# Both attentions take the second token tile's units first and the first token tile's units last

## The chip, the core and the metric

The kernel runs on one core of a Trainium2 chip. The metric is the device time of one execution, in microseconds (us). TensorE (PE) multiplies matrices, VectorE (DVE) does elementwise work and reductions, ScalarE (ACT) does activations and copies out of PSUM, and SyncE (SP) issues the loads of weights. Every engine takes its instructions in program order and waits on semaphores for the others.

## The reference, cut to what matters

Two blocks of a transformer run one after the other on 256 tokens of width 1024. The first block has a mixer of two attentions (a forgetting attention with 8 heads, "fox", and a sparse attention with the branches "cmp", "slc" and "win" over 2 groups of 4 heads) and a feed-forward layer that retrieves experts. The second block has a banded attention with 16 heads and sinks, and a gated delta rule. Both attentions work on blocks of 128 queries and are causal:

```python
def block(i):                       # i = 0, 1: 128 queries each
    q0 = i * Q_BLOCK
    logits = einsum(q[q0:q0+128], k) * scale + (c_t - c_s)   # fox
    p = softmax(where(k_pos <= q_pos, logits, NEG_INF))
    return einsum(p, v)
out = lax.map(block, jnp.arange(S_ // Q_BLOCK))

# second block: keys within 128 positions, 16 meta tokens, and a sink logit
p = softmax(concat([s_band - slope * dist, s_meta - slope * dist, sink]))
o = p_band @ v_band + p_meta @ v_meta
```

No block of queries depends on another, so their order is free.

## The kernel before

The 256 tokens are two tiles of 128 (`NT` is 2). A unit of `attention_stage` is one token tile, one kind and one group of heads: for each tile two fox units (four heads each), one cmp unit (eight heads, 15 keys), and slc, win, slc, win (four heads each). That makes 14 units, numbered u = 0 to 13. The first tile can see only 128 keys, the second tile 256. So a fox, slc or win unit of the first tile has 128x512 scores, called a **short unit** here, and one of the second tile 128x1024, a **long unit**. A cmp unit has 128x120 in either tile.

Each engine runs a hand-written pipeline over the units.

- PE, at index u: the scores of unit u+2 (L734 and L739 for fox, L746 for slc and win, L728 for cmp); the merge tile u (L232 with the weights' high part, 16 matmuls, and L236 with the low part, 8), which is a piece of another projection with a weight tile of its own; the values of unit u-1 (L778; fox and win units only, a win unit's for all three branches); and the turning (transpose) of unit u (L763, L758 for cmp).
- DVE: peaks(u) is the masked copy out of PSUM (L835, for cmp L831 before it), the maximum (L839) and its negative (L845); scale(u-1) is a reciprocal and products (L859, L865, L873); then the low part of a weight tile (L192, in `make_low`).
- ACT: four exponentials of unit u (L895), the high part of that weight tile (L180, in `make_high`), the copy of the merge tile out of PSUM (L314), the copy of the values (L917, `store`), and the copy of the turned unit u-1 (L907, L904 for cmp).

The waits that matter are these. The exponentials wait for peaks(u). `make_high` comes behind them on ACT, and it also waits until PE has used the high part of merge tile u-1, because the high and low parts have two buffers each. `make_low` waits for `make_high`, and peaks(u+1) comes behind `make_low` on DVE. So one step of the pipeline is a loop from DVE to ACT and back to DVE, and PE joins it by the use of the merge tile.

The stage ends when the last values are stored. Then all engines pass to `merge_stage` (L976, L989), which needs the output of all units.

`sink_attention_stage` has 16 units, one per token tile and pair of heads, with 144 keys in the first tile and 272 in the second. Its pipeline is the same in kind: scores L1627, half of a gate tile L275, values L1652, turning L1639; peaks L1680 to L1693 and scale L1699 to L1704; exponentials L1721 and L1724, copies L1732 and L1735, store L1605, and the gates' opening L1610. A weight tile's halves are made in every second unit. It shares its program block with `out_rows` (L3095), so engines go on without a barrier.

Of the kernel before, what the change touches and what calls it, by code (L numbers as in the profile page):

```python
# [20 lines left out]
NT = S // P  # L21
# [20 lines left out]
AH = 16  # L42
# [636 lines left out]
def attention_stage(k):  # L679
# [8 lines left out]
    ahead = [k.tiles["merge_rest"] + i for i in range(AHEAD, rest)] + list(early(k, "branch"))  # L688
    fill = ps[:, 7, 0:S]
    units = []  # L690
    for tt in range(NT):
        units += [(tt, "fox", 0), (tt, "fox", 1), (tt, "cmp", 0)]
        units += [(tt, b, g) for g in range(2) for b in ("slc", "win")]
    n_exp = [0]
# [880 lines left out]
def sink_attention_stage(k):  # L1575
# [10 lines left out]
    high, low = k.pair(L)  # L1586
    fill = ps[:, 7, 0:L]
    value_bank = lambda u: 6
    units = [(tt, a) for tt in range(NT) for a in range(AH // 2)]
    keys = lambda tt: META + (tt + 1) * P  # L1590
    soft, pt = k.soft2, k.pt2
    st = k.small[:, 0:24].rearrange("p (s a h) -> p s a h", s=2, a=6)
# [289 lines left out]
def second_block(k, stop):  # L1882
# [21 lines left out]
    with k.joined():  # L1904
        last_values = sink_attention_stage(k)
        k.split_early.add(k.tiles["attn_out"])
        opened, stored = k.signals["gate_opened"], k.signals["att_stored"]
        out_rows(k, "attn_out",
                 [(k.hm, 0, META, 0)] + [(k.h[:, tt, :], 2 + 2 * tt, P, META + tt * P) for tt in range(NT)],
                 k.y2, k.tiles["dn_in"] + RING, k.T2[:, 10:18, :], lambda q: opened.at(q + 1), following="dn_in",  # L1910
                 scale=[None] + [k.norms[:, 24 + 3 + tt:24 + 4 + tt] for tt in range(NT)],
                 gate_on=lambda q: stored.at(8 + 2 * q + 2), rest_by_scalar=last_values)
# [1037 lines left out]
def first_block(k, stop):  # L2950
# [29 lines left out]
    end_early(k, "merge_rest")  # L2980
    if stop <= 3: return
    attention_stage(k)
    end_early(k, "branch")
    if stop <= 4: return
# [242 lines left out]
```

## Time and profile before

| what | value |
|---|---|
| time, median of 3 runs (lowest, highest) | 1673.17 us (1672.14, 1673.53) |
| the profiled execution's own time | 1672.73 us |
| span in the profile | 1671.0 us |
| mean granted TensorE clock | 0.991 |
| PE busy | 1609.6 us (96%) |
| DVE busy | 1169.1 us (70%) |
| ACT busy | 906.4 us (54%) |
| first attention, from the first scores to the last store | 114.7 to 205.5 us |
| second attention, from the first scores to the last store | 1175.4 to 1241.7 us |

The profile is one execution. Its times count from the first instruction, and 1.7 us of the execution lie outside the span. A granted clock of 1.00 is TensorE's full 2.4 GHz, 0.50 is its lower level of 1.2 GHz.

### The profile page before, as it was taken

The numbers are of one execution on the slowest core, as the hardware profiler recorded it, in microseconds if no ns is written. First come the engines' busy times: TensorE is split into PE (matmuls) and PEld (weight loads), VectorE is DVE, ScalarE is ACT, GpSimd is POOL, SyncE is SP. The second block draws the span as 40 slices with busy tenths as digits, with TensorE's granted clock in tenths as the row PEclk, the third lists the DMA queues.
The fourth block names the chain that finished last, engine by engine and source line by source line (L and its number), as shares of the span: only waits on it lengthen the run. The fifth ranks groups of instructions, "written<-read, shape, count | busy, mean of one in ns | idle before, by whom it ended". The sixth has DMA issues, their size and how long they took to land. (4 is left out here: it accounts for less than half of the span.)

```text
span 1671.0 us, 33887 instructions
## 1 busy us (share of the span) xinstructions
PE 1609.6 (96%) x12980; PEld 1437.5 (86%) x12980; DVE 1169.1 (70%) x2011; ACT 906.4 (54%) x1621; POOL 74.1 (4%) x41
## 2 busy tenths in 40 slices
PE   7989899999999999999999999999999999999998
PEld 6888788999999999998888888887667889888877
DVE  5656666688988999986666666655765757756565
ACT  4336654455555776666656666653564655334543
POOL 0000000200000000000000000000001333200000
PEclk9979999999999999999999999999999999999999
DMA  6532254455555444446666666642222444310004
GB/s 216 186 114 89 79 174 151 156 186 164 182 183 164 139 129 138 135 133 201 192 197 189 193 195 190 195 141 86 76 69 84 150 150 155 104 38 3 3 31 147
DMA packets 63222, 230.02 MB, mean 138 GB/s; under 512 B 7024, under 2 KB 7280, under 8 KB 63104
## 3 DMA queue, kind: packets, MB, share of 16 engines
q1 hardware_dynamic: 63104, 228.37, 43.7%
q8 instruction: 83, 1.36, 0.3%
q14 instruction: 35, 0.29, 0.1%
HBM read 227.30 MB, written 1.05 MB: 137 GB/s over the span
## 5 line engine op out<-in xcount | busy, mean ns | idle before, releaser
L1097 DVE TENSOR_TENSOR tile_low<-weights,tile_high 128x1024 fp32r<-128x1024 f32 x252 | 307.9, 1222 | 141.4 <-ACT tile_high L1087 141.3
L1087 ACT ACTIVATE tile_high<-weights 128x1024 fp32r<-128x1024 f32 x252 | 268.1, 1064 | 134.0 <-issue 134.0
L180 ACT ACTIVATE tile_high<-weights 128x1024 fp32r<-128x1024 f32 x169 | 178.4, 1057 | 231.3 <-issue 56.6
L192 DVE TENSOR_TENSOR tile_low<-weights,tile_high 128x1024 fp32r<-128x1024 f32 x146 | 179.7, 1233 | 140.7 <-ACT tile_high L180 128.6
L1169 PE MATMUL banks<-parts,tile_high 128*128 128x256 f32 x2048 | 272.0, 286 | 0.9 <-ACT tile_high L1087 0.6
L1169 PEld LDWEIGHTS banks<-parts,tile_high 128*128 128x128 f32 x2048 | 255.5, 193 | 1.7 <-issue 1.7
L1489 PE MATMUL banks<-tile_high,parts 128*128 128x512 f32 x1024 | 253.0, 389 | 0.9 <-ACT parts L1447 0.9
L1489 PEld LDWEIGHTS banks<-tile_high,parts 128*128 128x128 f32 x1024 | 192.2, 188 | 40.9 <-issue 1.1
L232 PE MATMUL banks<-parts,tile_high 128*128 128x272 f32 (+1 forms) x1216 | 169.8, 293 | 4.4 <-PEq L2909 3.4
L232 PEld LDWEIGHTS banks<-parts,tile_high 128*128 128x128 f32 x1216 | 158.4, 192 | 14.1 <-issue 10.8
L1174 PE MATMUL banks<-parts,tile_low 128*128 128x256 f32 x1024 | 144.3, 284 | 4.1 <-DVE tile_low L1097 4.0
L1489 PE MATMUL banks<-tile_low,parts 128*128 128x512 f32 x512 | 136.8, 389 | 0.0
L1174 PEld LDWEIGHTS banks<-parts,tile_low 128*128 128x128 f32 x1024 | 132.0, 192 | 5.3 <-DVE tile_low L1097 5.3
L1489 PEld LDWEIGHTS banks<-tile_low,parts 128*128 128x128 f32 x512 | 96.1, 188 | 19.9
L1223 ACT ACTIVATE big<-banks 128x256 f32 (+1 forms) x71 | 47.1, 664 | 104.4 <-PE banks L1174 104.4
L236 PE MATMUL banks<-parts,tile_low 128*128 128x272 f32 (+1 forms) x608 | 87.9, 287 | 1.6 <-DVE tile_low L192 1.6
L1447 ACT ACTIVATE parts<-big 128x256 fp32r (+1 forms) x128 | 88.1, 689 | 0.0
L1239 ACT ACTIVATE rows<-rows,kept 128x128 f32<-128x128 f32 x256 | 80.1, 390 | 8.7 <-DVE rows L1343 8.7
L1508 DVE TENSOR_TENSOR parts<-big,parts 128x256 fp32r<-128x256 f32 x128 | 82.4, 644 | 1.8 <-ACT parts L1447 1.8
L236 PEld LDWEIGHTS banks<-parts,tile_low 128*128 128x128 f32 x608 | 80.4, 189 | 1.8 <-DVE tile_low L192 1.8
L1343 DVE TENSOR_TENSOR rows<-const,kept 128x1024 f32<-128x1024 f32 x64 | 76.9, 1218 | 0.0
L3095 PE MATMUL banks<-tile_high,parts 128*128 128x512 f32 (+1 forms) x288 | 71.3, 392 | 1.9 <-ACT parts L3027 1.9
(401 smaller groups left out, 2182.4 us busy)
## 6 DMA issues: line engine op xcount, KB each, us to landing
weights<-in_peer_u SPq DMA_DIRECT2D x128, 512.0 KB, 3.5
weights<-in_peer_v SPq DMA_DIRECT2D x128, 512.0 KB, 3.5
weights<-in_dn_in SPq DMA_DIRECT2D x49, 512.0 KB, 3.5
weights<-in_in_t SPq DMA_DIRECT2D x19, 512.0 KB, 3.5
weights<-in_attn_t SPq DMA_DIRECT2D x19, 512.0 KB, 3.5
weights<-in_in_m SPq DMA_DIRECT2D x16, 512.0 KB, 3.6
weights<-in_wq SPq DMA_DIRECT2D x16, 512.0 KB, 3.5
weights<-in_dn_out SPq DMA_DIRECT2D x16, 512.0 KB, 3.5
```

The costliest lines, as they stand in the source:

```text
L180: k.nc.scalar.activation(k.high[:, m % 2, :], k.ring.view(n), ACT.Copy).then_inc(*k.high_made.up())
L192: unit.tensor_tensor(k.low[:, m % 2, :], k.ring.view(n), k.high[:, m % 2, :].bitcast(F32), ALU.subtract).then_inc(*k.low_made[engine].up())
L232: ins = nc.tensor.matmul(out, high[:, c, :], rhs(c)[part], start=part + c == 0, stop=False)
L236: ins = nc.tensor.matmul(out, low[:, c, :], rhs(c)[0], start=False, stop=c == chunks - 1)
L1087: k.nc.scalar.activation(k.high[:, (s + j) % 2, :], k.ring.buf[:, j % RING, :], ACT.Copy).then_inc(k.high_made.sem, 1)
L1097: k.nc.vector.tensor_tensor(k.low[:, (s + j) % 2, :], k.ring.buf[:, j % RING, :], k.high[:, (s + j) % 2, :].bitcast(F32), ALU.subtract).th ...
L1169: ins = nc.tensor.matmul(ps[:, bank, 0:S], high[:, c, :], x[:, c, :], start=part + c == 0, stop=False)
L1174: ins = nc.tensor.matmul(ps[:, bank, 0:S], low[:, c, :], k.pair(S)[0][:, c, :], start=False, stop=c == KC - 1)
L1239: nc.scalar.activation(hot, hot, ACT.Copy, scale=k.chosenT[:, 2, Q * g + q:Q * g + q + 1]).then_inc(*scaled.up())
L1447: nc.scalar.activation(stage[:, j % STAGES, :], c_of(i, j), ACT.Copy).then_inc(staged.sem, 1)
L1489: ins = nc.tensor.matmul(ps[:, 4 + 2 * tt + half, :], c[:, j % STAGES, tt * P:tt * P + P], v[:, half, :], start=head and j + part == 0, st ...
L1508: nc.vector.tensor_tensor(stage_low[:, j % STAGES, :], c_of(i, j), stage[:, j % STAGES, :].bitcast(F32), ALU.subtract).then_inc(staged_low ...
```

## The change

In both stages the list of units is built with the token tiles in reverse. Everything else is unchanged: the same instructions with the same shapes, the same merge and gate tiles at the same index u, the same buffers and waits.

```diff
@@ attention_stage
-    for tt in range(NT):
+    for tt in reversed(range(NT)):
         units += [(tt, "fox", 0), (tt, "fox", 1), (tt, "cmp", 0)]
         units += [(tt, b, g) for g in range(2) for b in ("slc", "win")]
@@ sink_attention_stage
-    units = [(tt, a) for tt in range(NT) for a in range(AH // 2)]
+    units = [(tt, a) for tt in reversed(range(NT)) for a in range(AH // 2)]
```

PE at the start of the first attention, before. L734 and L739 are the scores of the two fox units, L728 those of the cmp unit, L232 and L236 merge tile 0, L763 the turning of unit 0.

```order
72 L734 MATMUL banks<-big 128x128 x4
73 L739 MATMUL banks<-big,const 128x128 x4
74 L734 MATMUL banks<-big 128x128 x4
75 L739 MATMUL banks<-big,const 128x128 x4
76 L728 MATMUL banks<-big 128x15 x8
77 L232 MATMUL banks<-parts,tile_high 128x256 x16
78 L236 MATMUL banks<-parts,tile_low 128x256 x8
79 L763 MATMUL banks<-const,big 128x128 x4
```

And after:

```order
72 L734 MATMUL banks<-big 128x256 x4
73 L739 MATMUL banks<-big,const 128x256 x4
74 L734 MATMUL banks<-big 128x256 x4
75 L739 MATMUL banks<-big,const 128x256 x4
76 L728 MATMUL banks<-big 128x15 x8
77 L232 MATMUL banks<-parts,tile_high 128x256 x16
78 L236 MATMUL banks<-parts,tile_low 128x256 x8
79 L763 MATMUL banks<-const,big 128x128 x8
```

The rows keep their places; the four groups of scores ahead of the first merge tile are now 256 keys wide, and the turning has eight matmuls for four.

PE in the middle of that stage, before. The merge tiles here are 5, 6 and 7; L778 x12 are the values of a win unit of the first tile, and the scores are those of the second tile's fox units and, last, of its cmp unit.

```order
100 L232 MATMUL banks<-parts,tile_high 128x256 x16
102 L778 MATMUL banks<-big 64x128 x12
103 L763 MATMUL banks<-const,big 128x128 x4
104 L734 MATMUL banks<-big 128x256 x4
106 L232 MATMUL banks<-parts,tile_high 128x256 x16
108 L763 MATMUL banks<-const,big 128x128 x4
109 L728 MATMUL banks<-big 128x15 x8
110 L232 MATMUL banks<-parts,tile_high 128x256 x16
112 L778 MATMUL banks<-big 64x128 x12
```

And after:

```order
100 L232 MATMUL banks<-parts,tile_high 128x256 x16
102 L778 MATMUL banks<-big 64x128 x20
103 L763 MATMUL banks<-const,big 128x128 x8
104 L734 MATMUL banks<-big 128x128 x4
106 L232 MATMUL banks<-parts,tile_high 128x256 x16
108 L763 MATMUL banks<-const,big 128x128 x8
109 L728 MATMUL banks<-big 128x15 x8
110 L232 MATMUL banks<-parts,tile_high 128x256 x16
112 L778 MATMUL banks<-big 64x128 x20
```

Here the wide values and turnings of the second tile now stand behind merge tiles 5 to 7, where those of the first tile stood, while the fox scores ahead of merge tile 6 are the narrow ones.

PE at the end of that stage, before: the last two merge tiles, the turning of units 12 and 13 (L763) and the values of the last two win units (L778).

```order
132 L232 MATMUL banks<-parts,tile_high 128x256 x16
133 L236 MATMUL banks<-parts,tile_low 128x256 x8
134 L778 MATMUL banks<-big 64x128 x20
135 L763 MATMUL banks<-const,big 128x128 x8
136 L232 MATMUL banks<-parts,tile_high 128x256 x16
137 L236 MATMUL banks<-parts,tile_low 128x256 x8
138 L763 MATMUL banks<-const,big 128x128 x8
139 L778 MATMUL banks<-big 64x128 x20
```

And after:

```order
132 L232 MATMUL banks<-parts,tile_high 128x256 x16
133 L236 MATMUL banks<-parts,tile_low 128x256 x8
134 L778 MATMUL banks<-big 64x128 x12
135 L763 MATMUL banks<-const,big 128x128 x4
136 L232 MATMUL banks<-parts,tile_high 128x256 x16
137 L236 MATMUL banks<-parts,tile_low 128x256 x8
138 L763 MATMUL banks<-const,big 128x128 x4
139 L778 MATMUL banks<-big 64x128 x12
```

The last turning and the last values have half and three fifths of their matmuls.

## Rows read from the trace of the kernel before

**Rows 1.** Busy time by stretch: us, then PE, PEld, DVE, ACT, POOL, PEclk, DMA.
```profile
152.89:191.34 38.45, 35.84 (x315) 30.86 (x316) 28.52 (x45) 24.80 (x63) 0.00 (x0) 1.00 0.27 83
```

**Rows 2.** Timeline, the steps: start, duration, engine, line, operation.
```profile
131.23 0.68 DVE L835 SCALAR_TENSOR_TENSOR big<-banks,big 128x512 f32<-128x512 f32 x1
136.65 0.68 DVE L835 SCALAR_TENSOR_TENSOR big<-banks,big 128x512 f32<-128x512 f32 x1
...
152.89 1.22 DVE L835 SCALAR_TENSOR_TENSOR big<-banks,big 128x1024 f32<-128x1024 f32 x1
...
159.81 1.22 DVE L835 SCALAR_TENSOR_TENSOR big<-banks,big 128x1024 f32<-128x1024 f32 x1
...
166.72 0.21 DVE L831 SCALAR_TENSOR_TENSOR big<-banks,big 128x60 f32<-128x60 f32 x1
...
170.60 1.22 DVE L835 SCALAR_TENSOR_TENSOR big<-banks,big 128x1024 f32<-128x1024 f32 x1
```

**Rows 3.** Timeline, the first attention's head and two later score groups.
```profile
119.45 0.69 DVE L835 SCALAR_TENSOR_TENSOR big<-banks,big 128x512 f32<-128x512 f32 x1 [0.69 <-PE banks L739]
...
121.16 3.62 PE L232 MATMUL banks<-parts,tile_high 128*128 128x256 f32 x16
...
126.09 0.72 PE L746 MATMUL banks<-big 64*128 64x128 f32 x8
...
127.09 0.21 DVE L831 SCALAR_TENSOR_TENSOR big<-banks,big 128x60 f32<-128x60 f32 x1
...
171.22 1.13 PE L746 MATMUL banks<-big 64*128 64x256 f32 x8
```

**Rows 4.** Busy time by stretch, around the fall and the rise of the clock.
```profile
110.00:112.00 2.00, 1.62 (x11) 1.30 (x10) 1.97 (x3) 0.75 (x3) 0.00 (x0) 0.69 0.78 258
...
122.00:124.00 2.00, 2.00 (x11) 2.00 (x11) 0.00 (x0) 0.76 (x4) 0.00 (x0) 0.50 0.00 0
124.00:126.00 2.00, 2.00 (x17) 1.93 (x16) 0.05 (x1) 1.14 (x2) 0.00 (x0) 0.89 0.00 0
```

**Rows 5.** Timeline, PE's pieces of a unit at full clock, one ACT row.
```profile
130.39 0.66 PE L763 MATMUL banks<-const,big 128*128 128x128 f32 x4
...
158.34 1.07 PE L728 MATMUL banks<-big 64*128 64x15 f32 x16
...
168.37 1.06 ACT L180 ACTIVATE tile_high<-weights 128x1024 fp32r<-128x1024 f32 x1 [0.21 <-PE banks L232]
...
170.20 1.09 PE L763 MATMUL banks<-const,big 128*128 128x128 f32 x8
...
190.48 2.18 PE L232 MATMUL banks<-parts,tile_high 128*128 128x256 f32 x16 [0.69 <-ACT big L314]
...
193.55 2.55 PE L778 MATMUL banks<-big 15*64 15x128 f32 x40
```

**Rows 6.** Timeline, the end of the first attention and the short counterparts.
```profile
126.20 0.60 ACT L907 ACTIVATE big<-banks 128x512 f32<-128x512 f32 x1
...
162.41 1.68 PE L778 MATMUL banks<-big 15*64 15x128 f32 x24
...
191.34 1.22 DVE L835 SCALAR_TENSOR_TENSOR big<-banks,big 128x1024 f32<-128x1024 f32 x1
...
201.44 1.02 ACT L907 ACTIVATE big<-banks 128x1024 f32<-128x1024 f32 x1 [0.46 <-PE banks L763]
...
205.12 0.39 ACT L917 ACTIVATE big<-banks 128x256 f32<-128x256 f32 x1 [2.65 <-PE banks L778]
```

**Rows 7.** Timeline, short and long copy and values of the second attention.
```profile
1195.24 0.38 ACT L1735 ACTIVATE big<-banks 128x256 f32<-128x256 f32 x1
...
1196.87 0.81 PE L1652 MATMUL banks<-big 16*64 16x128 f32 x8
...
1236.40 0.60 ACT L1735 ACTIVATE big<-banks 128x512 f32<-128x512 f32 x1
...
1240.35 1.02 PE L1652 MATMUL banks<-big 16*64 16x128 f32 x12 [1.17 <-ACT big L1735]
```

## The prediction

> **What bounds the kernel now.** I read the page first: TensorE is busy 96% of the span, but the change touches only the two attentions, 91 us and 66 us of it, so what counts is what ends last inside them. The view of busy time by stretch shows for the long units of the first attention 35.84 us of PE and 28.52 us of DVE in 38.45 us [rows 1]. Neither is idle for long and neither is full. Then I read the timeline of DVE for the distance between the starts of the masked copies, since each of them opens a step. A short step is 5.42 us (131.23 to 136.65), a long step 6.92 us (152.89 to 159.81), a cmp step 4.14 us in the first tile (127.09 to 131.23) and 3.88 us in the second (166.72 to 170.60) [rows 2, 3]. These equal lengths are the loop from DVE to ACT and back: masked copy, maximum, negative, four exponentials, high part, low part. So this loop is the bound in nearly all steps. PE runs beside it with little room. At the second tile's cmp unit ACT's high part waits 0.21 us for the merge tile's matmuls [rows 5], so there PE is already the later of the two.
>
> **The steps between head and tail.** The loop of unit u has only unit u's own copy, maximum and exponentials in it; scale(u-1) runs on DVE while ACT does exponentials. So a step costs by its own unit wherever it stands, and reversing the tiles permutes the sum. What doesn't permute are the ends: which unit stands where the clock is low, which one is last, and where PE's load collects.
>
> **The head of the first attention.** TensorE's granted clock is 0.50 from about 110.8 us to 124.4 us: the stretch 110 to 112 has a mean of 0.69, 122 to 124 has 0.50, 124 to 126 has 0.89 [rows 4]. The four fox score groups of units 0 and 1 fall into it. The trace has no 256-key group at half clock. At full clock a group with 128 keys takes 0.72 us and one with 256 keys 1.13 us, both rows of L746 [rows 3]; the extra 0.41 us is columns alone. At worst it doubles to 0.82 us, at best it stays 0.41 us, so the four cost between 1.6 and 3.3 us. I take 3.3, since the clock row says half speed. The start of peaks(1) then moves from 119.45 to 122.8. It is followed by a full long step, so peaks(2) starts at 122.8 + 6.9 = 129.7. Before, that was 127.09 [rows 3], because ACT's high part waited for the slow merge tile 0 (3.62 us, from 121.16), and a short step would have ended at 124.9. The wait that was there before swallows a part of the change. The head costs +2.6 us. PE's own path, 3.3 us later than before but with its last part at full clock, arrives at about the same time.
>
> **The middle.** From 129.7: the long cmp unit 3.88, four long steps 27.7, the two short fox steps 10.8, then peaks of the first tile's cmp unit at 172.1. By the loop alone peaks(10) would start 4.14 later, at 176.3. But here PE's load collects. Merge tile 12 started 0.86 us ahead of peaks(13), with no scores left ahead of it (190.48 against 191.34 [rows 5, 6]). In the new order merge tile 6 stands in the same place behind long units, with two narrow fox score groups ahead of it (1.4 us), and peaks(7) is at 161.3; so it starts at about 161.8. Up to merge tile 8 PE has two merge tiles of 3.07 us (190.48 to 193.55), the cmp scores 1.07, the last long win unit's values 2.55, one long turning 1.09, one short one 0.66, and a narrow score group 0.72 [rows 3, 5]. That is 12.2 us, about 12.0 as the pieces overlap by a few hundredths each. Merge tile 8 starts at 173.8 and its high part is used at 176.0. ACT's high part can only then begin, and from there to the next masked copy it is 2.23 us (168.37 to 170.60 [rows 2, 5]), which makes 178.2. So the first tile's cmp step is 1.9 us late: PE ends last there. After it the short steps need of PE 3.07 + 0.72 + 0.66 and half of 1.68 us of values (a win unit is every second one), 5.3 us against a loop of 5.42, so PE doesn't bound them. Three more short steps bring peaks(13) to 194.5, where it was 191.34 [rows 6]: +3.1 us.
>
> **The tail of the first attention.** Before, from peaks(13) to the end of the last store there are 191.34 to 205.51, 14.2 us [rows 6]. In it unit 13's pieces are in series. They become short: copy, maximum and exponentials -1.50 (6.92 less 5.42), turning -0.43 (1.09 to 0.66), ACT's copy -0.42 (1.02 to 0.60), values -0.87 (2.55 to 1.68) [rows 5, 6]. The sum is -3.2 us. The last merge tile, the same as before, remains in it. So the stage gives +3.1 - 3.2 = -0.1 us.
>
> **The second attention.** It has eight short and eight long units too, and its steps permute in the same way. The tail is what changes: the last copy 0.60 to 0.38 us, and the last values 1.02 to 0.81 us; out_rows stands behind these on PE, and PE waited 1.17 us for just this copy [rows 7]. That is -0.4 us. The head has only two score pairs of extra columns at low clock and DVE is then the longer one; I put it at 0, with half a microsecond either way.
>
> **Everything else** keeps its instructions and waits. SP's loads are released by the use of the same weight tiles at the same index, and move with them by a few microseconds at most.
>
> **The sum.** -0.1 - 0.4 = -0.5 us against the profiled execution's 1672.73 us gives 1672.2 us. That execution is 0.4 us under the median of the runs, 1673.17, and inside their spread. About 0.2% (3.3 us) is what a measurement of this kernel can tell from no change, so this forecast is no change.
>
> **The low clock, by work or by time.** The rows show the half clock lasting through four score groups, the cmp scores and most of merge tile 0, and ending at 124.4 [rows 3, 4]. If it ended after an amount of work, the new head would carry 3.3 us more of half-clock work, merge tile 0 would be used at about 128.1, and the head would be 0.6 us later than summed: 1672.8 us. The Trainium skill, in "TensorE: Matmul & The Clock Gate", section "Part 1: The HAM clock gate (the "warmup" mystery)", says that the slow phase is an amount of time and not a number of matmuls, and that it differs from run to run by where the hardware's free-running window stands. By that rule the end stays at 124.4 and the sum stays at 1672.2. No row here separates the two.
>
> **Rivals.**
>
> *A new thin stretch lets the clock fall ahead of the merge stage (slower).* The place is 195 to 206 us. PE has fewer turnings and values there in the new order, then waits for the last copy, the last store and the stage's end. If the clock falls as it did at 110.8, the merge stage starts at half clock for the same 13.6 us. The same shape, L232 x16, took 3.62 us there against 2.18 us at full clock [rows 3, 5], so 40% of 13.6 us is lost: +5.4 us, 1677.6 us. It decides from the point where the granted clock between 205 and 220 is below 1. For it: the clock did fall once in this part of the program. Against it: the old tail has the same waits, longer ones, and the short units fill PE more densely than the long ones did there.
>
> *PE catches up early (faster).* If PE isn't late at the cmp unit (-1.9), and the wide scores cost only their full-clock columns (1.6 in place of 3.3, -1.7), the tail's gain comes through: 1672.2 - 3.6 = 1668.6 us. For it: cmp waited only 0.2 us for PE before. Against it: the wide values and turnings all lie ahead of it now, and the half clock is in the rows.
>
> *PE stays late through the short half.* If the short steps take 5.9 us in place of 5.42, since scores, turning and values in PE's row wait for one another, the five of them behind the first tile's fox units cost +2.4: 1674.6 us. For it: that much PE work in a step leaves nearly no room. Against it: the steps in the trace of before are 5.42 to the hundredth in the short half, right behind the low clock, where PE was just as late.
>
> **How the numbers follow.** Forecast 0.70, PE late through the short half 0.12, PE early 0.10, clock falls 0.08. The range takes in the head's two bounds, the late PE and most of the early one: 1669.0 to 1675.6 us. Faster by over 0.2% 0.12, within 0.2% 0.78, slower 0.10: the rivals at 1668.6 and 1677.6 and a little more on each side.
>
> **What would show it.** The masked copies on DVE start near 122.8 (unit 1), 129.7 (unit 2), 161.3 (unit 7), 172.1 (unit 9), 178.2 (unit 10) and 194.5 (unit 13). The cmp step of the first tile is near 6 us and ACT's high part in it waits for L232. The last store ends near 205.4, and 11 us behind the last masked copy. The last values of the second attention start near 1239.9 where they started at 1240.35 [rows 7]. The forecast is wrong if the stage ends more than 2 us off, or if the granted clock falls where it was 1.00.

## The result and the profile after

The changed kernel took 1678.62 us (median of 8 runs, 1677.52 to 1680.13) against 1672.66 us before (8 runs beside them, 1670.90 to 1675.50). The ratio is 1.0029 with a 95% interval of 1.0017 to 1.0040: slower by 0.29%, where I had forecast no change at 1672.2 us and a range up to 1675.6 us. The profiled execution took 1677.52 us with a span of 1675.8 us, 4.8 us over the span before. Its mean granted clock is 0.986 (0.991 before).

Four differences make up the 4.8 us. From its first score matmul to its last store the first attention takes 93.6 us in place of 90.8: +2.8. From that store to the first L3095 it is 28.4 us in place of 26.4: +1.9. Between the end of L1489 and the first L1627 it is +1.4, and ahead of the first attention -1.4. The second attention adds nothing in this pair. Ahead of the first attention the two kernels are the same, so the -1.4 is a difference between two executions. The +1.4 is a stretch at low clock, which shows in the view of busy time by stretch, first of before and then of after:

```profile
1116.00:1118.00 2.00, 2.00 (x18) 2.00 (x17) 0.47 (x2) 0.47 (x1) 0.00 (x0) 1.00 0.00 0
```
```profile
1116.00:1118.00 2.00, 2.00 (x12) 2.00 (x10) 1.09 (x3) 1.15 (x3) 0.00 (x0) 0.50 0.63 244
```

The clock is 0.50 there from 1115.5 to 1119.0 us in the changed kernel.

The timeline of DVE in the changed kernel shows the masked copies that open the steps (they answer to [rows 2, 3, 6]); columns are start, duration, engine, line, operation.

```profile
117.42 1.23 DVE L835 SCALAR_TENSOR_TENSOR big<-banks,big 128x1024 f32<-128x1024 f32 x1 [4.45 <-PE banks L739]
121.44 1.23 DVE L835 SCALAR_TENSOR_TENSOR big<-banks,big 128x1024 f32<-128x1024 f32 x1 [1.33 <-PE banks L739]
129.88 0.21 DVE L831 SCALAR_TENSOR_TENSOR big<-banks,big 128x60 f32<-128x60 f32 x1
135.29 1.22 DVE L835 SCALAR_TENSOR_TENSOR big<-banks,big 128x1024 f32<-128x1024 f32 x1
...
162.93 0.68 DVE L835 SCALAR_TENSOR_TENSOR big<-banks,big 128x512 f32<-128x512 f32 x1
...
173.76 0.21 DVE L831 SCALAR_TENSOR_TENSOR big<-banks,big 128x60 f32<-128x60 f32 x1
...
179.75 0.68 DVE L835 SCALAR_TENSOR_TENSOR big<-banks,big 128x512 f32<-128x512 f32 x1
...
196.00 0.68 DVE L835 SCALAR_TENSOR_TENSOR big<-banks,big 128x512 f32<-128x512 f32 x1
```

Counted from the stage's first matmul (113.29; 114.7 before), unit 2 opens at 16.6 us in place of 12.4. Its step, the long tile's cmp, takes 5.41 us (129.88 to 135.29) where it was 3.88. The first tile's cmp step takes 5.99 us (173.76 to 179.75), where it was 4.14. The last step opens at 82.7 us in place of 76.6, and the tail is 10.9 us in place of 14.2.

PE, ACT and DVE in the head of the changed kernel, from the timeline:

```profile
113.29 2.08 PE L734 MATMUL banks<-big 64*128 64x256 f32 x8 [0.94 <-PEq L2909]
...
121.32 1.89 PE L728 MATMUL banks<-big 64*128 64x15 f32 x16
...
123.14 3.78 PE L232 MATMUL banks<-parts,tile_high 128*128 128x256 f32 x16
...
126.72 1.91 PE L236 MATMUL banks<-parts,tile_low 128*128 128x256 f32 x8
...
127.01 1.06 ACT L180 ACTIVATE tile_high<-weights 128x1024 fp32r<-128x1024 f32 x1 [0.77 <-issue]
...
128.73 1.23 DVE L192 TENSOR_TENSOR tile_low<-weights,tile_high 128x1024 fp32r<-128x1024 f32 x1 [3.27 <-PE banks L236]
...
133.05 1.06 ACT L180 ACTIVATE tile_high<-weights 128x1024 fp32r<-128x1024 f32 x1 [1.73 <-PE banks L232]
```

A wide score group takes 2.08 us at half clock. Merge tile 0 runs at half clock to its end, 128.63. ACT's high part starts only 0.09 us behind the end of its high part (126.92), with ACT idle for 0.77 us before it. DVE is idle for 3.27 us ahead of its low part. For most of that it waits for ACT's high part, done at 128.07; the last 0.6 us are the wait for merge tile 0's low part (L236). In the next step ACT waits 1.73 us for merge tile 1: PE is the late one there.

Busy time by stretch in the changed kernel, around the clock's rise and around the stage's end (columns as in [rows 1, 4]):

```profile
127.00:128.00 1.00, 1.00 (x7) 1.00 (x6) 0.00 (x0) 0.99 (x1) 0.00 (x0) 0.50 0.00 0
128.00:129.00 1.00, 1.00 (x6) 1.00 (x6) 0.27 (x1) 0.40 (x2) 0.00 (x0) 0.50 0.00 0
129.00:130.00 1.00, 1.00 (x9) 0.83 (x9) 1.00 (x2) 0.22 (x2) 0.00 (x0) 0.95 0.00 0
...
206.00:207.00 1.00, 0.50 (x10) 0.26 (x6) 0.00 (x0) 0.39 (x1) 0.00 (x0) 1.00 0.00 0
207.00:208.00 1.00, 0.00 (x0) 0.00 (x0) 0.00 (x0) 0.78 (x1) 0.00 (x0) 0.80 0.00 0
208.00:209.00 1.00, 0.58 (x3) 0.62 (x4) 0.70 (x1) 1.00 (x2) 0.00 (x0) 0.50 0.77 102
...
213.00:214.00 1.00, 1.00 (x6) 1.00 (x6) 0.00 (x0) 0.66 (x1) 0.00 (x0) 0.50 0.00 0
214.00:215.00 1.00, 1.00 (x9) 1.00 (x8) 0.67 (x1) 0.00 (x0) 0.00 (x0) 0.79 0.00 0
```

The clock rises at 129.1 us, 15.8 us into the stage (9.7 before), and it falls again at 207.6 and stays at 0.50 until 214.4, where it had been 1.00 before. The merge stage's first matmuls run in it, as the timeline of PE shows; the end of the tail stands above them:

```profile
204.82 1.68 PE L778 MATMUL banks<-big 15*64 15x128 f32 x24 [0.69 <-ACT big L907]
208.41 4.10 PE L976 MATMUL banks<-parts,tile_high 128*128 128x256 f32 x16 [1.92 <-ACT parts L989]
212.31 1.91 PE L982 MATMUL banks<-parts,tile_low 128*128 128x256 f32 x8
```

Sixteen L976 take 4.10 us here and 2.08 us two tiles later (217.07). The last values wait 0.69 us for ACT's last copy (1.11 us before) and are short, as forecast.

The second attention's values in the view of one line, before and after (count, shortest, median and longest in ns, first and last start). The first L1627 starts at 1175.5 before and 1180.2 after, so the last of these comes 65.6 us into the stage in both.

```profile
L1652 PE MATMUL banks<-big x160: 268/273/324, 1182.8 to 1241.1; 128*64 128x128 f32 x96, 16*64 16x128 f32 x64
```
```profile
L1652 PE MATMUL banks<-big x160: 268/273/324, 1189.7 to 1245.8; 128*64 128x128 f32 x96, 16*64 16x128 f32 x64
```

### The profile page after: what moved, and what is told of

It is laid out like the page before. It is cut to its first block and busy times, and to the rows that moved or that the text cites. A ratio compares the mean times of both kernels' runs of the same rounds, so it can differ in the third digit from the quotient of the medians.

```text
span 1675.8 us, 33887 instructions
## 1 busy us (share of the span) xinstructions
PE 1614.9 (96%) x12980; PEld 1441.6 (86%) x12980; DVE 1169.5 (70%) x2011; ACT 907.0 (54%) x1621; POOL 74.1 (4%) x41
## 5 line engine op out<-in xcount | busy, mean ns | idle before, releaser
L1489 PE MATMUL banks<-tile_high,parts 128*128 128x512 f32 x1024 | 253.0, 389 | 0.9 <-ACT parts L1447 0.9
L1489 PEld LDWEIGHTS banks<-tile_high,parts 128*128 128x128 f32 x1024 | 192.2, 188 | 40.8 <-issue 1.1
L232 PE MATMUL banks<-parts,tile_high 128*128 128x272 f32 (+1 forms) x1216 | 170.0, 293 | 4.8 <-PEq L2909 3.4
L232 PEld LDWEIGHTS banks<-parts,tile_high 128*128 128x128 f32 x1216 | 158.4, 192 | 14.0 <-issue 10.4
L1489 PE MATMUL banks<-tile_low,parts 128*128 128x512 f32 x512 | 136.8, 389 | 0.0
L1489 PEld LDWEIGHTS banks<-tile_low,parts 128*128 128x128 f32 x512 | 96.1, 188 | 19.9
L236 PE MATMUL banks<-parts,tile_low 128*128 128x272 f32 (+1 forms) x608 | 89.4, 290 | 1.6 <-DVE tile_low L192 1.6
L236 PEld LDWEIGHTS banks<-parts,tile_low 128*128 128x128 f32 x608 | 81.9, 192 | 1.8 <-DVE tile_low L192 1.8
L3095 PE MATMUL banks<-tile_high,parts 128*128 128x512 f32 (+1 forms) x288 | 71.3, 392 | 1.9 <-ACT parts L3027 1.9
```

The costliest lines, as they stand in the source:

```text
L232: ins = nc.tensor.matmul(out, high[:, c, :], rhs(c)[part], start=part + c == 0, stop=False)
L236: ins = nc.tensor.matmul(out, low[:, c, :], rhs(c)[0], start=False, stop=c == chunks - 1)
L1489: ins = nc.tensor.matmul(ps[:, 4 + 2 * tt + half, :], c[:, j % STAGES, tt * P:tt * P + P], v[:, half, :], start=head and j + part == 0, st ...
L3095: ins = nc.tensor.matmul(ps[0:rows, bank + half, :], xs[:, place(q), c0:c0 + rows][:, c, :], w[:, c, :], start=q + part + c == 0, stop=q = ...
```

## The experiments

All ratios are to the kernel before, timed in turn on the same chip. Executions of one and the same kernel spread over 2 to 11 us here (the kernel before over 5 to 7), and profiles show low-clock stretches in different places, so a ratio and its interval come first and one profile second. Line numbers in the profiles of the experiments are shifted by the lines that an edit adds or takes away. "Head" is the time from the stage's first matmul to the masked copy of unit 2, "tail" that from the last masked copy to the last store, "gap" that from there to the first L3095.

### The reversal in one attention at a time

```diff
 attention_stage          e1:  for tt in reversed(range(NT))     e2: unchanged
 sink_attention_stage     e1:  unchanged                         e2: reversed(range(NT))
```

> The reversal in the first attention alone. Theory A (the cost is the first attention's own: its head at the low clock, its cmp units, and the clock falling again ahead of the merge stage): first scores to last store 93.6 us as with both changes (90.8 before), granted clock 0.50 for some microseconds behind 207 us, time +4 to +6 us over before. Rival B (half of the cost belongs to the second attention or to what lies between them, as the 1.4 us that both changes lost between 1104 and 1180 us): time only +2 to +3 us. Rival C (the added low clock is chance and would hit any kernel): time within 1.5 us of before.

> The reversal in the second attention alone. Theory A: time within 1 us of before; from the first L1627 to the last L1652 65.6 us as in both kernels, the shorter tail paid for by the wider scores in the head. Rival B: +2 to +3 us, the rest of the cost. My forecast's step for this stage was -0.4 us.

e1 gave 1.0039 (1.0026 to 1.0052), which is 6.5 us, a little over what theory A said; e2 gave 1.0001 (0.9991 to 1.0012). The profile of e1 repeats the changed kernel's: head 16.6, stage 93.7, tail 10.9, gap 28.4, and the same fall of the clock behind 207 us. In e2 the second attention takes 65.3 us and everything ahead of it is as before; behind it the clock is at 0.50 from 1240.8 to 1244.2 us, where it was 1.00 before, and the rest of the program is 1.5 us longer. e3 and e5 below show the same behind the reversed second attention, and so does e12 behind the unchanged one; the changed kernel's own profile doesn't. Whether the reversal brings it is open. By e2's ratio the second reversal costs 2.0 us at most.

So the cost comes with the first reversal, and rivals B and C fall as far as they put it down to the second one or to chance. But the 1.4 us between L1489 and L1627 come back in e1, whose second attention is unchanged: the clock is at 0.50 from 1115.7 to 1119.1 us. e7 below has such a stretch too (1114.5 to 1118.0); the other eleven profiles, before among them, have none between 1100 and 1170 us. These three kernels are ones in which the clock falls ahead of the merge stage. Whether the one brings the other, and by what, no run takes apart.

### Idle time around the stage's end filled

```diff
 attention_stage, PE, after the loop over units
+            pe.wait_ge(*gated.last())
+            keep_busy(k, 7, 1)
 merge_stage, PE, ahead of the loop over c
+            keep_busy(k, 7, 2)
```

> Both reversals, and idle time of PE around the stage's end filled with matmuls that no result uses (one at the end of the attention stage, two at the start of the merge stage, 128x384 each). Theory A: the clock stays at 1.00 from 200 to 220 us, the stretch from the last store to the first L3095 is back from 28.4 to 26.5 us, and the time 2 us under the changed kernel's. Rival (the fall is set by something other than PE's idle time in the tail, for instance by the thin matmuls of the last values): the clock falls all the same and the time is as with both changes or 0.5 us longer for the added matmuls.

> The kernel before with the same three added matmuls: the control for them. Theory A: the clock did not fall there before, so they bring nothing and cost 0 to 0.6 us. Rival (the clock falls there in a part of the executions of before too, and the profile only happened to show one in which it didn't): the median falls by 0.5 to 2 us and its spread narrows.

e3 gave 1.0025 (1.0016 to 1.0035), e4 1.0010 (1.0001 to 1.0019). In e3's profile the clock is 1.00 across the stage's end and the gap is 26.9 us: the two stretches by two microseconds show it, first of e1 and then of e3, whose stage ends 3.2 us later.

```profile
206.00:208.00 2.00, 0.63 (x12) 0.39 (x8) 0.00 (x0) 1.04 (x2) 0.00 (x0) 0.94 0.00 0
208.00:210.00 2.00, 1.45 (x5) 1.21 (x6) 1.56 (x2) 1.98 (x3) 0.00 (x0) 0.50 0.77 215
```
```profile
208.00:210.00 2.00, 1.87 (x25) 1.53 (x26) 0.45 (x1) 0.22 (x2) 0.00 (x0) 1.00 0.00 0
210.00:212.00 2.00, 1.70 (x6) 0.71 (x5) 0.00 (x0) 1.31 (x3) 0.00 (x0) 1.00 0.18 16
```

So the fall there comes with PE's thin tail and goes with the filling; the control shows that the filling itself costs 0.5 us of gap (26.9 against 26.4). By e4's ratio it is 1.7 us (0.2 to 3.2), more than the 0 to 0.6 us expected. e3's median, 1678.37 us, is hardly under the changed kernel's 1678.62 and e1's 1679.02, timed beside it. By the ratios e3 is 2.3 us under e1, with intervals that overlap: the expected 2 us aren't shown in the times. Its 12 runs fall in two groups, five between 1674.7 and 1675.4 and seven between 1677.5 and 1680.6. The profiled one, of the slower group, shows the clock fall inside the stage instead, behind a wait of PE for DVE:

```profile
149.72 1.12 PE L236 MATMUL banks<-parts,tile_low 128*128 128x256 f32 x8
152.53 1.09 PE L763 MATMUL banks<-const,big 128*128 128x128 f32 x8 [1.69 <-DVE big L875]
...
155.62 3.78 PE L232 MATMUL banks<-parts,tile_high 128*128 128x256 f32 x16
```

The clock is at 0.50 from 153.9 to 160.7 us, and once more from 200.0 to 201.6. The stage takes 96.4 us. Whether this explains the whole slower group is open, since only one of its runs has a profile.

The same profile shows how far the head depends on the moment at which the clock rises. Up to the stage's end e3's instructions in the first attention are those of the changed kernel (timeline, and busy time by stretch):

```profile
123.70 3.42 PE L232 MATMUL banks<-parts,tile_high 128*128 128x256 f32 x16
...
129.44 0.21 DVE L833 SCALAR_TENSOR_TENSOR big<-banks,big 128x60 f32<-128x60 f32 x1
```
```profile
126.00:127.00 1.00, 1.00 (x8) 1.00 (x8) 0.02 (x1) 0.79 (x4) 0.00 (x0) 0.73 0.00 0
```

The clock rises at 126.5 us, 2.8 us behind the start of merge tile 0, where it was 6.0 in the changed kernel and in e1. With that the head is 15.6 us (16.6 there) and the long cmp step 5.00 us (5.41 there).

### Merge tile 0 ahead of the first scores

```diff
+            merge_tile(pe, k, MERGE_FIRST, fill)
             scores(0)
             scores(1)
             for u in range(len(units) + 1):
...
-                if u < rest:
+                if 1 <= u < rest:
```

> Both reversals, and merge tile 0 issued ahead of the first scores in the first attention (same instructions, other order on PE). Theory A (the wide scores do not bring the clock up, and the dense merge tile does): the clock rises within about 7 us of the stage's first matmul and not after 15.8 us, the four wide score groups fall largely in full clock (1.13 us each and not 2.08), and the stage, first matmul to last store, is 2 to 3 us shorter than 93.6 us. Rival (the low stretch ends by time or by chance): the rise stays near 129 us, the scores are only pushed back by the merge tile, 5.7 us at half clock, and the stage is 1 to 3 us longer.

> The kernel before with merge tile 0 ahead of the first scores. Theory A: the clock rises earlier than 9.7 us into the stage, 6 to 7 us, but the first scores come 5.7 us later; the stage is within 1.5 us of 90.8. Rival: the rise stays at 9.7 us, and the stage is 2 us longer.

e5 gave 1.0042 (1.0028 to 1.0055), e6 1.0016 (1.0007 to 1.0025). The first half of theory A holds: in both the clock rises 5.7 us into the stage, and three of e5's four wide groups take 1.13 us. The second half fails: the stages take 96.1 us (e5) and 93.2 us (e6), longer than 93.6 and 90.8, and both are outside what was expected. PE has no merge tile left to run while it waits for the first exponentials, sits idle for 3.6 us, and the clock falls again, from the timeline of e5:

```profile
122.30 1.13 PE L739 MATMUL banks<-big,const 8*128 8x256 f32 x8
123.36 1.07 PE L728 MATMUL banks<-big 64*128 64x15 f32 x16
128.02 1.97 PE L763 MATMUL banks<-const,big 128*128 128x128 f32 x8 [3.59 <-DVE big L874]
```

Eight turnings take 1.97 us, at half clock. The clock stays low from 126.1 to 133.0 us. The head is 17.3 us, no shorter than 16.6. In e6 PE is idle for 2.06 us in the same place, and the clock falls at 122.7. The merge tile in its old place covers that wait. In e5 the clock also falls at 197.8 us, inside the stage, and at 211.5, ahead of the merge stage, behind the same short tail as in the changed kernel.

### A mixed order, and the candidate for a better version

```diff
-    units = []
-    for tt in range(NT):
-        units += ...
+    short, long = (lambda *kinds: [(0, b, g) for b, g in kinds]), (lambda *kinds: [(1, b, g) for b, g in kinds])
+    fox, sparse = [("fox", 0), ("fox", 1)], [("slc", 0), ("win", 0), ("slc", 1), ("win", 1)]
+    units = short(*fox) + long(("cmp", 0), *sparse) + long(*fox) + short(("cmp", 0), *sparse)
```

> First attention only, another order: the two short fox units, the long cmp, slc, win, slc, win, the long fox units, then the short cmp, slc, win, slc, win. The head's scores are as narrow as before, the tail is the short one. Theory A: the head costs what it did before (peaks of unit 2 12.4 us into the stage), the tail from the last masked copy to the last store is 10.9 us and not 14.2, the short cmp step may be up to 1.9 us late; stage 89.3 to 91.3 us. If the clock then falls ahead of the merge stage, as with both changes, the time is +1 to +2 us over before, if not -1.5 to 0. Rival (the tail's 3.2 us are given back in any order by PE's load): stage 91 us or more.

> The mixed order with the three added matmuls around the stage's end. Theory A: clock 1.00 from 200 to 220 us, time -1.5 to 0 us against before, the best of all orders. Rival: as the mixed order without them.

e7 gave 1.0017 (1.0005 to 1.0028), e8 1.0003 (0.9994 to 1.0013). The timeline of DVE of e7, whose stage starts at 114.87 us, shows the masked copies of unit 2 and unit 13:

```profile
127.28 0.21 DVE L830 SCALAR_TENSOR_TENSOR big<-banks,big 128x60 f32<-128x60 f32 x1
...
195.28 0.69 DVE L834 SCALAR_TENSOR_TENSOR big<-banks,big 128x512 f32<-128x512 f32 x1
```

Head 12.4 us, as before; tail 10.9 us; stage 91.3 us in both, which is the upper end of theory A and within the rival's. So the extra head of the changed kernel comes with the wide fox units at its start. The middle gives back the tail's 3.3 us: the last step opens at 80.4 us where it was 76.6. Of these 3.8 us, 1.5 are the order's own, since a long step now stands ahead of the last one in place of a short one. The two cmp steps give 1.7 (4.56 us for the long one, 5.12 for the short one) and two short steps of 5.75 and 5.71 us give 0.6.

In e7 the clock falls ahead of the merge stage too, at 206.6 us (gap 28.3); in e8 it doesn't (26.9). The stage and the gap make 2.4 us, and e7's ratio says 2.8 (0.8 to 4.7). Its profiled span is 4.7 us longer than that of before: besides these 2.4 us it has 1.4 us more between L1489 and the first L1627, and 0.9 in the second attention, which is unchanged. The medians are 1675.82 (e7) and 1674.20 (e8), with 1673.77 for before.

### What brings the clock up

```diff
 e9                              e10
+            scores(0, False)   +            keep_busy(k, 7, 4)
+            scores(1, False)
             scores(0)                       scores(0)
             scores(1)                       scores(1)
```

> The kernel before with the score groups of units 0 and 1 issued twice, the first time without a signal: PE runs some 4.9 us more of the same narrow score matmuls ahead of merge tile 0. Theory A (the clock comes up behind the dense merge tile and not behind the scores): the low stretch gets longer, the rise comes 14 us or more behind the stage's first matmul (9.7 before), 3 to 6 us behind the start of merge tile 0. Rival (it comes up by time since PE became busy, as I had summed): the rise stays 9 to 11 us behind the first matmul, that is, before or at the start of merge tile 0.

> The kernel before with four 128x384 matmuls that no result uses ahead of the first scores, about 4.5 us of dense work at half clock in place of the repeated scores. Theory A: the rise comes earlier relative to the scores, at 7 to 8 us behind the stage's first matmul, during the scores. Rival (by time): 9 to 11 us behind the first matmul. Both: the stage is longer than 90.8 us by about the added work less what the clock gives back, +2 to +4 us.

Both are the kernel before with about 5 us of PE work more ahead of the scores (`keep_busy` issues 128x384 matmuls that no result uses). e9, timeline of PE and busy time by stretch:

```profile
112.05 1.23 PE L734 MATMUL banks<-big 64*128 64x128 f32 x8 [0.94 <-PEq L2912]
...
120.12 1.22 PE L739 MATMUL banks<-big,const 8*128 8x128 f32 x8
...
123.09 3.78 PE L232 MATMUL banks<-parts,tile_high 128*128 128x256 f32 x16
```
```profile
120.00:122.00 2.00, 2.00 (x18) 1.66 (x16) 1.28 (x3) 1.26 (x7) 0.00 (x0) 0.50 0.00 0
...
126.00:128.00 2.00, 2.00 (x12) 2.00 (x11) 0.00 (x0) 1.04 (x1) 0.00 (x0) 0.50 0.00 0
128.00:130.00 2.00, 2.00 (x17) 1.71 (x17) 1.31 (x2) 1.00 (x3) 0.00 (x0) 0.84 0.00 0
```

PE ran scores without a gap for 11 us, from 112.05 to 123.09, and the clock stayed at 0.50. It rose at 128.6, 5.5 us behind the start of merge tile 0. e10:

```profile
113.94 5.46 PE L295 MATMUL banks<-const 128*128 128x384 f32 x8 [0.94 <-PEq L2910]
119.33 0.92 PE L734 MATMUL banks<-big 64*128 64x128 f32 x8
...
123.11 3.69 PE L232 MATMUL banks<-parts,tile_high 128*128 128x256 f32 x16
```
```profile
118.00:119.00 1.00, 1.00 (x3) 0.25 (x1) 0.00 (x0) 0.00 (x0) 0.00 (x0) 0.50 0.22 86
119.00:120.00 1.00, 1.00 (x9) 0.67 (x8) 0.00 (x0) 0.00 (x0) 0.00 (x0) 0.60 0.01 4
...
123.00:124.00 1.00, 1.00 (x8) 0.97 (x7) 0.93 (x3) 1.00 (x6) 0.00 (x0) 0.60 0.00 0
```

Here it rose at 119.8, 5.9 us behind the first added matmul, and with nothing but the same scores after it, it fell again at 123.2 although PE had no gap. Both outcomes are theory A's (the rise slightly earlier than it said), and the rival's, 9 to 11 us in both, is met by neither. The times: e9 1.0033 (1.0020 to 1.0045), e10 1.0007 (0.9996 to 1.0018). Eight score groups, the cmp scores and the whole of merge tile 0 run at half clock in e9, and its median is 4.9 us above before. e10's 5.4 us of added work cost 2.8 us of stage in its profile and 1.2 us (-0.7 to 3.0) by the ratio. There is one profile of each.

### The head's waits filled

```diff
 prepare_stage, PE
             ins.then_inc(*turned.up())
+            keep_busy(k, 1, 1)
             pe.wait_ge(*vec.at(15))
             nc.tensor.matmul(ps[:, 6, 0:2 * N_CMP], k.c("perm"), k.kcmp, ...).then_inc(*turned.up())
+            keep_busy(k, 1, 1)
```

> The kernel before with one unused 128x384 matmul in each of two waits of PE just ahead of the first attention (112 to 115 us). Theory A: the clock, low from 110.8 us, comes up one level change sooner, about 121 us, the head is 1 to 2 us shorter, and the time 0.5 to 1.5 us under before. Rival (the matmuls delay the last products of the stage before and the clock keeps its course): +0.5 to +1.5 us.

> The mixed order with the added matmuls both in the head's waits and around the stage's end: the candidate for a version that beats both. Theory A: 0.5 to 2 us under before. Rival: as the mixed order with the tail filled, within 1 us of before.

e12 has these two matmuls, the mixed order and the three matmuls around the stage's end. e11 gave 1.0017 (1.0008 to 1.0026) and e12 1.0018 (1.0009 to 1.0027), 2.8 and 3.0 us: the rivals' side, and more than they said. The clock did not come up sooner but 11.6 us into the stage (9.7 before), 5.1 and 5.2 us behind the start of merge tile 0. The head is 13.1 us in both, 0.7 longer, with the same narrow scores as before. Nothing that I tried beats the kernel before; e8 is level with it.

## Why the prediction was wrong

**What bounds it, and the steps.** Right outside the cmp steps: the loop's steps are 6.91 and 5.41 us in the new places.

**The head (forecast +2.6, measured +4.2).** This is the step that failed. The four wide score groups cost what I took: 2.08 us each, 1.22 us before, so peaks(1) comes 3.4 us later. What failed is "PE's own path ... with its last part at full clock". I held the rise fixed in time at 124.4, so that merge tile 0 would be mostly in full clock. The clock rose 15.8 us into the stage in place of 9.7: merge tile 0 starts 3.4 us later behind the wide scores, and the rise came 6.0 us behind its start and not 3.3. So the tile ran at half clock to its end, 128.6. ACT's high part came 0.8 us late by it and DVE's low part another 0.6. I weighed the rise "by work" and priced it at only 0.6 us more, because I followed the tile's high part and left out its low part, which make_low waits for as well.

The 4.2 us have two parts. e7 shows that the extra comes with the wide units at the head, and e9 shows with narrow scores that more score work ahead of the tile moves the rise back too. But the moment of the rise behind the tile's start also differs between executions: 3.2 to 3.4 us with a head of 12.3 to 12.4 (before, e2, e4, e7, e8), 5.1 and 5.2 with 13.1 (e11, e12); with wide scores 2.8 with a head of 15.6 (e3), 6.0 with 16.6 (the changed kernel and e1). Heads with a like rise differ by 3.2 and 3.5 us. So some 3.2 to 3.5 us go with the wide scores, and 0.7 to 1.0 us with the moment of the rise; whether the change sets that moment is open. The 2.6 us of the forecast would have been short with either rise.

**The rule that I weighed.** The Trainium skill, in "TensorE: Matmul & The Clock Gate", section "Part 1: The HAM clock gate (the "warmup" mystery)", has the slow phase as an amount of time whatever is issued. The trace doesn't agree here: with PE busy from 112.05 us on, the clock stayed low for 11 us of scores (e9), and it came up 5.5 us behind the start of merge tile 0 (e9) and 5.9 us behind that of the added matmuls (e10). The measurement decides.

**The long cmp unit (forecast 0, measured +1.5).** PE's lateness from the head is still there in the next step, and ACT waits 1.73 us for merge tile 1. I had looked for PE's load only at the second cmp unit. It is the same term of the sum as the head, one step on. In e3, with the earlier rise, it is 1.1.

**The middle.** Right: the first tile's cmp step was forecast 6.1 us (172.1 to 178.2) and took 5.99. The high part of merge tile 8 ends at 177.43 and ACT's high part starts at 177.52, as the forecast has it. PE didn't bound the short steps after it (5.42 each). The rival in which PE stays late through the short half is out.

**The tail.** Right in size: 14.2 to 10.9 us, forecast 11.0. But it was costed as if it were free of consequence. The stage's sum is +2.8 in place of -0.1: 1.6 from the head, 1.5 from the long cmp step, and -0.2 from the other steps and the tail.

**The gap behind it.** The slow rival came true in its place, with a smaller price: the clock fell at 207.6 us for 6.8 us, not 13.6, and cost 1.9 us, not 5.4. I gave it 0.08, with the argument that the old tail waits longer. The waits are no longer than they were (0.69 and 1.92 us now, 1.11 and 1.92 before), so PE's idle time alone doesn't explain it; the work between them is thinner too, 24 narrow matmuls of values for 40. It fell in the changed kernel, e1, e5 and e7, all four profiles with the short tail and unfilled, and in none of the seven with the long tail or the three with the short tail and filled waits. That a short tail brings it is borne out by e7 (its only other change is in the middle), and that filling takes it away by e3, e8 and e12, each in one profile. Why exactly the short tail lets it fall and the long one doesn't stays open.

**The second attention (forecast -0.4, measured 0).** e2 has it at 1.0001 (0.9991 to 1.0012) and 65.3 us for 65.6, which fits either number. The low clock behind it in e2, e3 and e5 (1.5 us in e2) was not in the sum.

**The sum.** +2.8 and +1.9 make 4.7 us, and the median moved by 6.0, the ratio by 4.9 (2.8 to 6.7). The stage's error alone would have given 1675.1 us, within my range; with the gap it is 1677.0. The +1.4 and -1.4 elsewhere cancel in the profiled pair, but they are not alike. The -1.4 stands ahead of the change. The +1.4 is there in the changed kernel, in e1 and in e7 and in no other profile, so it may be part of the cost, and its cause stays open.

## What to carry to other kernels

A reordering that leaves a chain's sum alone is decided at its two ends: see what stands where the clock is low, and what PE has left to do where the stage hands over. Follow each tile that a slow engine delays to all of its waiters, not the first one. The moment at which the clock rises in one profile is not fixed: e3 has the same head as the changed kernel and a rise 3.1 us sooner after the stage's start. A shorter tail on the critical path is worth its length only if the engine behind it arrives with its clock up; look at the granted clock of the next stage before you book the gain.

## What the runs showed of the hardware that I had not expected

TensorE's clock, once at 0.50, stayed there through 11 us in which PE ran the fp32 score matmuls (64 and 8 rows) without a gap (e9), and fell to it from 1.00 while they and merge tile 0's first matmuls ran without a gap (e10, at 123.2 us). It rose 5.5 us behind the start of merge tile 0 in e9 and 5.9 us behind the first added 128x384 matmul in e10. In the eleven profiles in which merge tile 0 stands behind the scores (all but e5, e6 and e10), the rise came 2.8 to 6.0 us behind its start, which lay 6.4 to 11.0 us into the stage. So PE busy at 1.00 was seen here at either level of the clock.
